# Retention's products in another order: pair of heads, block of keys, head

## The chip, the core and the metric

The kernel runs on one core of a Trainium2 chip, in one launch. A core has TensorE (matrix products), VectorE, ScalarE, GpSimd and SyncE, which work side by side and wait for each other by semaphores. The metric is the device time of one execution in microseconds. Of the kernel before there are three timed runs, and one execution more that the hardware profiler recorded.

## The reference, cut to what matters

The program computes four layers of a small language model over 512 tokens with 1024 features, in float32. The first two layers mix the tokens in three ways: retention (4 heads), an attention over selected keys, called dsa (4 heads), and a dilated attention (8 heads). Only retention is touched:

```python
RET_HEADS, HEAD_DIM = 4, 64
inner = jnp.einsum('bhncd,bhnmd->bhncm', qc, kc) * decay[None, :, None]
inner = jnp.einsum('bhncm,bhnme->bhnce', inner, vc)
...
cross = jnp.einsum('bhncd,nbhde->bhnce', qc, state_prev) * xi[None, :, None, :, None]
o = inner + cross
...
mu = jnp.mean(o, axis=-1, keepdims=True)
var = jnp.mean(jnp.square(o - mu), axis=-1, keepdims=True)
o = (o - mu) * lax.rsqrt(var + NORM_EPS) * norm_w.astype(jnp.float32)
```

For each head this is a causal product of queries with keys, times a decay that falls with the distance of the two tokens, times the values, and then a norm over the head's 64 features. The kernel computes it without the chunks: all queries that come at or after a block of 128 keys, times that block, at once.

## The kernel before, in words

Features lie on the 128 partitions and tokens along them. Two heads of 64 features share the 128 partitions: of retention's rotated queries and keys (`retqk`) head h has partitions 0 to 63 for even h and 64 to 127 for odd h, of block h // 2.

One unit of retention is a head h and a block kb of 128 keys. It goes through three steps:

- score product (line 1176, TensorE, semaphore `ret_s`): keys of the block times all queries from the block on. It uses 64 rows of TensorE's array (the head's 64 partitions) and all 128 columns. Its width w is 512 − 128 kb: 512, 384, 256 or 128. The result goes to PSUM bank 4 or 5 in turns.
- decay step (line 1480, VectorE, semaphore `ret_p`): the score times the decay table, into one of four buffers `ret_st`.
- value product (line 1184, TensorE, semaphore `ret_o`): values of the block times that buffer, accumulated over the blocks in PSUM bank 6 or 7. It uses all 128 rows and 64 columns of the array: the result has the head's 64 partitions.

Both products are in float32, and the trace shows two instructions (and two weight loads) for each. Everything else large is split into a high and a low part in a reduced format (fp32r), where a product is one instruction; line 750 (the attention's scores) and line 306 (weights times features) are of that kind.

The list `ru` (line 1062) sets the order of the 16 units. It is fixed, and all engines go through it. Retention runs beside the dsa attention, in its steps i = 6 to 14. A step of that attention on TensorE is: scores for two units in every second step (line 750), a transposition of probabilities (line 769), then what `retention(i)` adds, then the products with values (line 780). `retention(i)` issues the score products of units 2(i − 6) and 2(i − 6) + 1, and then the value products of the two units before them. VectorE's part of a step is the attention's masking (lines 823 and 829), in some steps a reciprocal and a scaling of finished results (lines 843 and 844), and then two decay steps. Retention's rotation (lines 1167, 1469, 1471) is ahead of it in steps 4 and 5, its norm in steps 15 to 17 behind it (lines 1190 and 1193). The weights come by SyncE's queue, and ScalarE and GpSimd split them (lines 260 and 269).

The waits of TensorE in this part: score product u waits for decay step u − 2, which frees its PSUM bank; value product u waits for decay step u. In both, one wait stands ahead of each product.

Of the kernel before, what the change touches and what calls it, by code (L numbers as in the profile page):

```python
# [14 lines left out]
TB = S // P  # L15
# [4 lines left out]
RET_H, DSA_H, DIL_H, FOX_H, IDX_H = 4, 4, 8, 8, 8  # L20
# [88 lines left out]
def build(nc, a, out):  # L109
    ctx = ExitStack()  # L110
    with ctx:
# [67 lines left out]
        def at(name, v):  # L179

            return sems[name], base[name] + v
# [868 lines left out]
        def first_layer(block, L):  # L1050
# [8 lines left out]
            out_a, out_b = Pace(16, 0, 3), Pace(16, 16, 7)  # L1059
            ROT, RET, GN = 4, 6, 15  # L1060
            units = [(qb, h) for qb in range(1, TB) for h in range(IDX_H)]
            ru = [(h, kb) for h in range(RET_H) for kb in range(TB)]

            @block.sync
            def _(sp):
# [26 lines left out]
            def _(pe):  # L1092
# [24 lines left out]
                for i in range(0, len(units), 2):  # L1117
                    qb, h = units[i]
# [40 lines left out]
                def retention(i):  # L1159
# [10 lines left out]
                    for u in (2 * (i - RET), 2 * (i - RET) + 1):  # L1170
                        if 0 <= u < len(ru):
                            h, kb = ru[u]
                            p0, w = HD * (h % 2), S - kb * P
                            if u >= 2:
                                pe.wait_ge(*at("ret_p", u - 1))
                            sg["ret_s"].by(pe.matmul(  # L1176
                                ps[:, 4 + u % 2, 0:w], retqk[p0:p0 + HD, 2 + h // 2, kb * P:(kb + 1) * P],
                                retqk[p0:p0 + HD, h // 2, kb * P:S], start=True, stop=True))
                    for u in (2 * (i - RET) - 2, 2 * (i - RET) - 1):
                        if 0 <= u < len(ru):  # L1180
                            h, kb = ru[u]
                            p0, w = HD * (h % 2), S - kb * P
                            pe.wait_ge(*at("ret_p", u + 1))
                            sg["ret_o"].by(pe.matmul(  # L1184
                                ps[p0:p0 + HD, 6 + h // 2, kb * P:S], retv[:, kb, h * HD:(h + 1) * HD],
                                st_b[u % 4][:, 0:w], start=kb == 0, stop=kb == TB - 1, skip_group_check=True))
# [10 lines left out]

                pe.wait_ge(*at("dq_low", 2))
                dsa.tensor(pe, retention)
                pe.wait_ge(*at("mix_lo", 6))  # L1200
                pe.wait_ge(*at("ret_lo", 2))
# [136 lines left out]
            def _(dve):  # L1338
# [121 lines left out]
                def retention(i):  # L1460
# [10 lines left out]
                            sg["ret_rotd"].by(dve.tensor_tensor(retqk[:, j, :], gn[j % 2][:], st_b[j][:], ALU.add))  # L1471
                            dve.wait_ge(*at("ret_rotd", j + 1))
                    for u in (2 * (i - RET), 2 * (i - RET) + 1):
                        if 0 <= u < RET_H * TB:
                            h, kb = divmod(u, TB)
                            w = S - kb * P
                            dve.wait_ge(*at("ret_s", u + 1))
                            if u >= 4:
                                dve.wait_ge(*at("ret_o", u - 3))
                            sg["ret_p"].by(dve.tensor_tensor(st_b[u % 4][:, 0:w], ps[:, 4 + u % 2, 0:w],  # L1480
                                                             rtab[:, T_DECAY + h * S:T_DECAY + h * S + w], ALU.mult))
# [16 lines left out]
                    if i == GN + 2:  # L1498
                        for j in range(2):
# [3 lines left out]
                                                              ALU.subtract))  # L1503

                dsa.vector(dve, retention)
                for m in range(4):
                    add_out(pl.out_b, m, 4 + m)
# [596 lines left out]
        with nc.Block() as block:  # L2104
            for L in range(DEPTH):
                first_layer(block, L)
            for layer in range(2):
                second_layer(block, layer)
# [21 lines left out]
```

## Time and profile before

| | us |
|---|---|
| timed runs | 2570.02, 2578.37, 2581.41 |
| their median | 2578.37 |
| the profiled execution | 2571.64 |
| its span in the trace | 2569.9 |
| TensorE busy | 2451.2 (95%) |
| VectorE, ScalarE, GpSimd busy | 1064.6, 944.7, 1005.7 |
| mean clock granted to TensorE | 0.975 of 2.4 GHz |

Retention's products run from 271 to 308 us of the span in the first layer and from 963 to 999 in the second. The trace's times are those of the profiled execution. A matrix product's recorded duration holds a tail in which the next one is already running, so durations of neighbours overlap and the distance of two starts says more than a duration. A granted clock of 0.50 is 1.2 GHz, 1.00 is 2.4 GHz.

### The profile page before, as it was taken

The page shows a single profiled execution, that of the slowest core. Times are in us where ns is not written, and L with a number is a line of the kernel's source. Part 1 is how long each engine was busy: PE and PEld are TensorE (multiplying, and loading weights), DVE is VectorE, ACT ScalarE, POOL GpSimd, SP SyncE. Part 2 cuts the span into 40 slices and gives each one's busy share as a digit, 9 for nine tenths or more (in the row PEclk, how much of TensorE's full clock was granted, in tenths as well). Part 3 has the DMA queues.
Part 4 walks back from the last instruction along what each step waited for, and adds up shares of the span by engine and source line. Part 5 has one row for each costly group of instructions (what it writes and reads, how often), then busy time and mean ns, then how long its engine had stood idle before and what let it go on. Part 6 is the DMA issues. An engine that isn't in the chain of part 4 may idle for free.

```text
span 2569.9 us, 29379 instructions
## 1 busy us (share of the span) xinstructions
PE 2451.2 (95%) x11844; PEld 1994.8 (78%) x11844; DVE 1064.6 (41%) x1931; ACT 944.7 (37%) x1306; POOL 1005.7 (39%) x789
## 2 busy tenths in 40 slices
PE   8988999999999889999999979899999898999997
PEld 6777588888877766888888768888888767888886
DVE  4766451221347664411224553632223766522224
ACT  5333352322343343522325333522223564422222
POOL 4422134444444230444445411354443524444442
PEclk9999899999999999999999979999999999999998
DMA  4212023233232120322323211132322312232331
GB/s 163 72 44 91 17 66 98 98 99 99 79 103 83 33 74 17 99 99 99 98 98 103 90 33 34 64 101 99 99 98 82 115 49 83 77 104 98 99 98 50
DMA packets 138279, 212.36 MB, mean 83 GB/s; under 512 B 7456, under 2 KB 65952, under 8 KB 137888
## 3 DMA queue, kind: packets, MB, share of 16 engines
q1 hardware_dynamic: 138144, 210.48, 24.7%
q8 instruction: 94, 1.54, 0.2%
q14 instruction: 41, 0.34, 0.0%
HBM read 208.36 MB, written 2.10 MB: 82 GB/s over the span
## 4 chain that ended last, share of the span: by engine, by line
PE 53%; DVE 5%; ACT 2%; issue 2%; POOL 0%; POOLq 0%; DVEq 0%; ACTq 0%
PE ps L306 45%; PE ps L331 4%; PE ps L780 1%; DVE x L653 1%; PE ps L1681 1%; PE ps L468 1%; PE ps L769 1%; DVE h_lo L543 1%; DVE tmp_both L648 0%; ACT w_hi L260 0%; PE ps L1176 0%; POOL w_lo L269 0%; PE ps L750 0%; PE ps L1184 0%; DVE ub L1899 0%
## 5 line engine op out<-in xcount | busy, mean ns | idle before, releaser
L269 POOL TENSOR_TENSOR w_lo<-raw,w_hi 128x512 fp32r<-128x512 f32 (+1 forms) x776 | 995.3, 1313 | 1528.1 <-ACT w_hi L260 1528.1
L306 PE MATMUL ps<-h_hi,w_hi 128*128 128x512 f32 x1696 | 681.2, 402 | 12.1 <-POOL w_lo L269 10.5
L306 PE MATMUL ps<-h_hi,w_lo 128*128 128x512 f32 x1696 | 663.3, 391 | 0.0
L306 PE MATMUL ps<-h_lo,w_hi 128*128 128x512 f32 x1696 | 663.3, 391 | 0.0
L260 ACT ACTIVATE w_hi<-raw 128x2048 fp32r<-128x2048 f32 (+2 forms) x196 | 363.5, 1855 | 729.1 <-PE ps L306 710.8
L306 PE MATMUL ps<-hid_hi,w_hi 128*128 128x512 f32 x992 | 392.3, 395 | 6.0 <-DVE hid_lo L851 5.1
L306 PE MATMUL ps<-hid_hi,w_lo 128*128 128x512 f32 x992 | 388.0, 391 | 0.0
L306 PEld LDWEIGHTS ps<-h_hi,w_hi 128*128 128x128 f32 x1696 | 319.5, 188 | 88.0 <-issue 21.0
L306 PE MATMUL ps<-hid_lo,w_hi 128*128 128x512 f32 x992 | 387.7, 391 | 0.0
L306 PEld LDWEIGHTS ps<-h_lo,w_hi 128*128 128x128 f32 x1696 | 319.3, 188 | 69.0 <-issue 5.6
L306 PEld LDWEIGHTS ps<-h_hi,w_lo 128*128 128x128 f32 x1696 | 319.1, 188 | 69.1 <-issue 0.4
L306 PEld LDWEIGHTS ps<-hid_hi,w_hi 128*128 128x128 f32 x992 | 187.5, 189 | 46.7 <-DVE hid_lo L851 6.3
L306 PEld LDWEIGHTS ps<-hid_hi,w_lo 128*128 128x128 f32 x992 | 187.2, 189 | 39.7
L306 PEld LDWEIGHTS ps<-hid_lo,w_hi 128*128 128x128 f32 x992 | 187.6, 189 | 38.2 <-issue 0.5
L1457 DVE TENSOR_TENSOR x<-x,ps 128x512 f32<-128x512 f32 x96 | 65.3, 685 | 290.5 <-PE ps L306 290.5
L863 ACT ACTIVATE p<-p,stat 128x128 f32<-128x128 f32 (+3 forms) x128 | 71.8, 561 | 239.0 <-DVE stat L829 238.7
L1528 DVE SCALAR_TENSOR_TENSOR tmp_both<-ps,rstd 128x512 f32<-128x512 f32 x64 | 44.1, 691 | 246.0 <-PE ps L306 222.8
L717 DVE TENSOR_TENSOR tmp_both<-ps,rstd 128x512 f32<-128x512 f32 x48 | 33.0, 690 | 247.8 <-PE ps L306 247.7
L769 PE MATMUL ps<-tab,p 128*128 128x128 f32 x320 | 64.1, 301 | 32.9 <-ACT p L863 16.9
L2089 DVE TENSOR_TENSOR acc<-acc,ps 128x512 f32<-128x512 f32 x64 | 43.8, 687 | 108.6 <-PE ps L306 108.6
L331 PE MATMUL ps<-hid_hi,w_hi 128*128 128x256 f32 x256 | 75.2, 294 | 4.3 <-issue 3.2
L823 DVE CUSTOM_DVE_ANT_0 p<-ps,tab 128x128 f32<-128x128 f32 (+3 forms) x104 | 49.3, 474 | 72.0 <-PE ps L757 30.5
(290 smaller groups left out, 2904.7 us busy)
## 6 DMA issues: line engine op xcount, KB each, us to landing
raw<-in_w_up SPq DMA_DIRECT2D x32, 1024.0 KB, 5.5
raw<-in_w_down SPq DMA_DIRECT2D x32, 1024.0 KB, 4.9
raw<-in_ffn_w_gate SPq DMA_DIRECT2D x44, 512.0 KB, 3.7
raw<-in_ffn_w_up SPq DMA_DIRECT2D x44, 512.0 KB, 4.7
raw<-in_w_in SPq DMA_DIRECT2D x20, 1024.0 KB, 4.9
raw<-in_ffn_w_down SPq DMA_DIRECT2D x20, 1024.0 KB, 4.9
raw<-in_w_out SPq DMA_DIRECT2D x8, 1024.0 KB, 4.9
raw<-in_ev_w_in SPq DMA_DIRECT2D x8, 1024.0 KB, 5.3
```

Of the source, the lines that this page charges most:

```text
L260: act.activation(w_hi[r][:, 0:slot.rows, 0:slot.width], raw[r][:, 0:slot.rows, 0:slot.width], ACT.Copy).then_inc(sems["hi_split"], 1)
L269: pool.tensor_tensor(w_lo[r][:, k, 0:slot.width], raw[r][:, k, 0:slot.width], w_hi[r][:, k, 0:slot.width].bitcast(F32), ALU.subtract).then ...
L306: mm = pe.matmul(o, lh, rh, start=first and q == 0, stop=last and q == 2, skip_group_check=True)
L331: mm = pe.matmul(o, lh, rh, start=first and q == 0, stop=last and q == 2, skip_group_check=True)
L468: mm = pe.matmul(ps[:, nm.bank, 0:S // 2], ones, two(nm.acc)[:, i, :], start=i == 0, stop=i == 1)
L717: sg["bank_free"].by(dve.tensor_tensor(o, src, rstd[:, 0:width], ALU.mult))
L769: mm = pe.transpose(ps[:, 2, kb * P:(kb + 1) * P], p_t[i % self.PB][:, kb * P:(kb + 1) * P], ident)
L823: sg["s_masked"].by(dve.tensor_tensor_reduce(out=p_t[i % self.PB][:, 0:w], in0=ps[:, e, 0:w], in1=self.bias(qb), scale=1.0, scalar=TAKEN, ...
L863: sg["p_ready"].by(act.activation(p_t[i % self.PB][:, 0:w], p_t[i % self.PB][:, 0:w], ACT.Exp, bias=sn[:, i:i + 1], scale=SCALE, accum_out ...
L1457: sg["bank_free"].by(dve.tensor_tensor(x[:, b, :], x[:, b, :], ps[:, HALF * st.groups[g].half + m, :], ALU.add))
L1528: sg["bank_free"].by(dve.scalar_tensor_tensor(out=tmp[n % 2][:], in0=ps[:, HALF * st.groups[g].half + m, :], scalar=0.0, in1=rstd[:], op0= ...
L2089: sg["bank_free"].by(dve.tensor_tensor(acc[:, b, :], acc[:, b, :], src, ALU.add))
```

## The change

The order of the units becomes pair of heads, block of keys, head. Before, head 0 went through its four blocks, then head 1, and so on: widths 512, 384, 256, 128, 512, ... Now heads 0 and 1 take turns: block 0 of head 0, block 0 of head 1, block 1 of head 0, and so on: widths 512, 512, 384, 384, ... Two neighbouring units then lie in different halves of the partitions. Each step of `retention(i)` still has two score products and two value products, now of one width each. The waits for the decay step stand only ahead of the first of the two, and ask for the later of the two numbers. VectorE takes its units from the same list instead of counting head by head.

```diff
-            ru = [(h, kb) for h in range(RET_H) for kb in range(TB)]
+            ru = [(h + e, kb) for h in range(0, RET_H, 2) for kb in range(TB) for e in range(2)]
...
                             h, kb = ru[u]
                             p0, w = HD * (h % 2), S - kb * P
-                            if u >= 2:
-                                pe.wait_ge(*at("ret_p", u - 1))
+                            if u >= 2 and u % 2 == 0:
+                                pe.wait_ge(*at("ret_p", u))
                             sg["ret_s"].by(pe.matmul(
                                 ps[:, 4 + u % 2, 0:w], retqk[p0:p0 + HD, 2 + h // 2, kb * P:(kb + 1) * P],
                                 retqk[p0:p0 + HD, h // 2, kb * P:S], start=True, stop=True))
...
                             p0, w = HD * (h % 2), S - kb * P
-                            pe.wait_ge(*at("ret_p", u + 1))
+                            if u % 2 == 0:
+                                pe.wait_ge(*at("ret_p", u + 2))
                             sg["ret_o"].by(pe.matmul(
                                 ps[p0:p0 + HD, 6 + h // 2, kb * P:S], retv[:, kb, h * HD:(h + 1) * HD],
                                 st_b[u % 4][:, 0:w], start=kb == 0, stop=kb == TB - 1, skip_group_check=True))
...
                     for u in (2 * (i - RET), 2 * (i - RET) + 1):
-                        if 0 <= u < RET_H * TB:
-                            h, kb = divmod(u, TB)
+                        if 0 <= u < len(ru):
+                            h, kb = ru[u]
                             w = S - kb * P
                             dve.wait_ge(*at("ret_s", u + 1))
```

TensorE's queue in steps 6 and 7 of the first layer, where retention's products begin (the change adds one line, so line 1184 is 1185 in the new numbering; an instruction's width is its second number, and a product stands as one row here):

```order
 L1176 MATMUL ps<-retqk 128x512 [waits ret_rotd]
-L1176 MATMUL ps<-retqk 128x384
+L1176 MATMUL ps<-retqk 128x512
 L780 MATMUL ps<-dsa_v,pT_84 128x64 [waits pT_copied]
 L780 MATMUL ps<-dsa_v,pT_84 128x64
 L769 MATMUL ps<-tab,p_79 128x128 [waits pT_copied,p_ready]
 L769 MATMUL ps<-tab,p_79 128x128 x2
-L1176 MATMUL ps<-retqk 128x256 [waits ret_p]
-L1176 MATMUL ps<-retqk 128x128 [waits ret_p]
-L1184 MATMUL ps<-ret_st_110,retv 64x512 [waits ret_p]
-L1184 MATMUL ps<-ret_st_111,retv 64x384 [waits ret_p]
+L1176 MATMUL ps<-retqk 128x384 [waits ret_p]
+L1176 MATMUL ps<-retqk 128x384
+L1185 MATMUL ps<-ret_st_110,retv 64x512 [waits ret_p]
+L1185 MATMUL ps<-ret_st_111,retv 64x512
```

The attention's rows stay where they are. Each of retention's places holds two products as before, now of one width and with one wait.

VectorE's queue in step 11, behind the reciprocal and the scaling. Before:

```order
357 L1480 TENSOR_TENSOR ret_st_112<-ps,rtab 128x256 [waits ret_o,ret_s]
358 L1480 TENSOR_TENSOR ret_st_113<-ps,rtab 128x128 [waits ret_o,ret_s]
359 L823 ISA p_78,stat<-ps,sc_95 128x384 [waits pT_ready,s_ready]
360 L823 ISA stat 128x1
361 L829 TENSOR_SCALAR stat<-stat 128x1 [waits s_masked]
```

The same place after the change:

```order
357 L1481 TENSOR_TENSOR ret_st_112<-ps,rtab 128x384 [waits ret_o,ret_s]
358 L1481 TENSOR_TENSOR ret_st_113<-ps,rtab 128x384 [waits ret_o,ret_s]
359 L823 ISA p_78,stat<-ps,sc_95 128x384 [waits pT_ready,s_ready]
360 L823 ISA stat 128x1
361 L829 TENSOR_SCALAR stat<-stat 128x1 [waits s_masked]
```

The two decay steps are wider here, and both stand ahead of the score product that TensorE issues next.

## Rows read from the trace of the kernel before

**Rows 1.** The page: busy time of each engine, us (share of the span), instructions.

```profile
PE 2451.2 (95%) x11844; PEld 1994.8 (78%) x11844; DVE 1064.6 (41%) x1931; ACT 944.7 (37%) x1306; POOL 1005.7 (39%) x789
```

**Rows 2.** Timeline of PE, second layer: start, length, instructions merged, idle before.

```profile
968.67 2.98 PE L1184 MATMUL ps<-ret_st,retv 128*64 128x512 f32 x4
...
984.75 0.92 PE L1176 MATMUL ps<-retqk 64*128 64x256 f32 x4
985.59 1.72 PE L1184 MATMUL ps<-ret_st,retv 128*64 128x512 f32 x4
987.24 1.10 PE L780 MATMUL ps<-dsa_v,pT 128*128 128x64 f32 x8
...
989.69 1.77 PE L1176 MATMUL ps<-retqk 64*128 64x512 f32 x4 [0.26 <-DVE ret_st L1480]
...
998.11 0.86 PE L1184 MATMUL ps<-ret_st,retv 128*64 128x256 f32 x4
...
1000.15 0.52 PE L769 MATMUL ps<-tab,p 128*128 128x128 f32 x3 [0.60 <-ACT p L863]
```

**Rows 3.** Stretches: start:end length, PE busy, granted clock, DMA share, GB/s.

```profile
271.40:295.30 23.90, 23.90 (x60) 0.50 0.14 44
...
964.30:971.10 6.80, 6.80 (x18) 0.51 0.47 154
971.10:999.00 27.90, 27.03 (x136) 1.00 0.00 1
```

**Rows 4.** Timeline of DVE in steps 6, 11 and 12; what DVE waited for at L1480.

```profile
274.15 0.56 DVE L1480 TENSOR_TENSOR ret_st<-ps,rtab 128x384 f32<-128x384 f32 x1 [0.59 <-PE ps L1176]
...
304.21 0.20 DVE L843 RECIPROCAL stat<-stat 128x8 f32<-128x8 f32 x1 [4.39 <-PE ps L780]
304.45 0.69 DVE L844 TENSOR_TENSOR on<-ps,stat 128x512 f32<-128x512 f32 x1
305.06 0.61 DVE L1480 TENSOR_TENSOR ret_st<-ps,rtab 128x256 f32<-128x256 f32 x2
...
306.68 1.20 DVE L1480 TENSOR_TENSOR ret_st<-ps,rtab 128x512 f32<-128x512 f32 x2 [0.36 <-PE ps L1176]
...
  PE ps L1176: 17.3, 15
```

**Rows 5.** Line 1176: what its engine sat idle for: us, times.

```profile
  DVE ret_st L1480: 1.5, 4
```

**Rows 6.** Timeline at retention's start, PE and its weight loads (PEld), both layers.

```profile
963.25 2.23 PE L1176 MATMUL ps<-retqk 64*128 64x512 f32 x4 [2.18 <-DVE retqk L1471]
...
271.12 2.99 PE L1176 MATMUL ps<-retqk 64*128 64x512 f32 x4 [2.18 <-DVE retqk L1471]
...
271.78 0.33 PEld L1176 LDWEIGHTS ps<-retqk 64*128 64x128 f32 x1 [0.36 <-issue]
...
272.63 0.33 PEld L1176 LDWEIGHTS ps<-retqk 64*128 64x128 f32 x1 [0.52 <-issue]
```

**Rows 7.** Timeline of PE and its weight loads in the first layer's step 12.

```profile
305.52 1.77 PE L1176 MATMUL ps<-retqk 64*128 64x512 f32 x4 [0.26 <-DVE ret_st L1480]
...
306.06 0.19 PEld L1176 LDWEIGHTS ps<-retqk 64*128 64x128 f32 x1 [0.24 <-issue]
...
306.49 0.19 PEld L1176 LDWEIGHTS ps<-retqk 64*128 64x128 f32 x1 [0.24 <-issue]
```

**Rows 8.** Groups by form, whole run: xcount, busy us, mean ns, idle before.

```profile
L1184 PE MATMUL ps<-ret_st,retv 128*64 128x512 f32 x16 | 11.3, 794 | 0.0
```

**Rows 9.** Timeline of PE: attention's score pairs (L750), whole-array products (L306).

```profile
252.01 0.40 PE L306 MATMUL ps<-hid_hi,w_lo 128*128 128x512 f32 x1
252.24 0.39 PE L306 MATMUL ps<-hid_hi,w_hi 128*128 128x512 f32 x1
...
267.46 0.39 PE L750 MATMUL ps<-hid_lo,dsaq_hi 64*128 64x512 f32 x2
267.69 0.40 PE L750 MATMUL ps<-hid_hi,dsaq_lo 64*128 64x512 f32 x2
```

## The prediction

> **What bounds the kernel now.** I read the page's busy times first: TensorE is busy 95% of the span and no other engine half of it [rows 1]. So a change to TensorE's own work counts in full, wherever TensorE is the engine waited for. The next view is the timeline of TensorE in the stretch where retention's products run. A step there is a run of products, one behind the other: in the second first_layer the products of scores with keys start at 984.75, those with values at 985.59, the attention's own products at 987.24, and between them nothing is idle [rows 2]. In the 27.9 us from 971.1 to 999 TensorE is busy for 27.03 [rows 3]. VectorE, which multiplies the decay in between, sits idle 17.3 us in all until a score product comes, while the score products sat idle for it only 1.5 us in both layers together [rows 4, 5]. So TensorE is what is waited for, and a step costs the time that its products stream.
>
> The view of stretches gives the clock. TensorE streams at half of its full speed (1.2 instead of 2.4 GHz) from 271.4 to 295.3 in the first layer's retention, and from 964.3 to 971.1 in the second's [rows 3]. Ahead of both lies an idle time of 2.18 us until VectorE has rotated the keys [rows 6]. The stretch from the first score product to the seventh pair of them is 305.52 − 271.12 = 34.4 us in the first layer and 989.69 − 963.25 = 26.4 us in the second [rows 2, 6, 7]: the same work, 8.0 us apart by the clock alone.
>
> **What a product costs.** Each float32 product is two instructions (16 instructions of each width on each of the two lines, for 8 products in two layers; one width stands) [rows 8]. Weight loads are issued as soon as the instruction ahead starts to stream, so their pitch is the streaming time. It is 306.49 − 306.06 = 0.43 us for 512 columns at full clock [rows 7] and 272.63 − 271.78 = 0.85 us at half clock [rows 6]. A product of 512 columns is 0.86 us, and narrower ones go down in proportion. A head has widths 512, 384, 256 and 128, 2.5 units of 512; four heads and two lines make 20 units a layer, 17.2 us at full clock.
>
> **The change, part by part.**
>
> *The order.* So far two neighbouring products belong to one head. They use the same 64 partitions of keys and queries (the score product) or the same 64 partitions of the result (the value product), and so the same half of the array: four instructions in a row, A0 A1 A0' A1'. Now the neighbours are heads h and h+1, in different halves: A0 A1 B0 B1, both of one width. Can B0 run beside A1? The trace shows it for the reduced-precision products of the attention's scores, whose two heads alternate between the same two halves: two products of 512 columns come every 267.69 − 267.46 = 0.23 us, where one product over the whole array comes every 252.24 − 252.01 = 0.23 us [rows 9]. Two for the time of one. There the order is A B A B, all pairs overlap. Here the two instructions of a head follow each other, A1 has to wait for A0 (0.43 apart above), and B0 is behind A1 in the queue. So of four unit times three are left: the saving is a quarter. For the value products, which split the array by its columns of results instead of its rows, no row shows an overlap. The bounds are nothing (float32 instructions of two halves do not overlap) and a half (B0 gets past A1, and all pairs overlap as in rows 9). I take the quarter: it is the overlap of rows 9 with the order in the queue that the weight loads of rows 7 show.
>
> The sum: a quarter of 17.2 is 4.3 us a layer, 8.6 in both. At half clock a unit costs double. The first layer's slow stretch holds score products 0 to 7 and value products 0 to 5, (2560 + 2176)/512 = 9.25 units; a quarter of 0.86 on top of each is 2.0 us. The second's holds score products 0 to 3 and value products 0 and 1, 4.25 units, 0.9 us. Together **11.5 us**.
>
> The Trainium skill says in "TensorE: Matmul & The Clock Gate", Part 3, that matmuls start and end strictly in program order, which gives the same three of four. The same part says that a weight load overlaps a running matmul only where the row group differs. This trace differs: the loads at 306.06 and 306.49 start while a product of the same rows streams, and no gap follows. If the rule held for value products, which all use all rows, they would not overlap; that is the rival "scores only" below, and its time is worked out from rows there.
>
> *The waits.* TensorE's score product u waited for VectorE's step u−2, and the value product u for step u. Now the first of a pair waits for the second's step too, and the second has no wait. The waits taken away were met already, but for fractions of a microsecond: TensorE's idle time before value products is 0 in the view by form, of which one width stands and the other three read alike [rows 8]. I put their removal at nothing. One wait gets stricter: score product 2k must wait for VectorE's step 2k−1, not 2k−2. Where does that show? In most steps TensorE has 1.7 us or more of value products and attention work between [rows 2]. At one step it doesn't: behind the attention's eighth value group VectorE does a reciprocal, 0.20, and a scaling, 0.69, and only then the two decay steps at 305.06, and TensorE starts at 305.52, after an idle time of 0.26 [rows 4, 7]. Now both steps must be done, and both are 384 wide instead of 256 and 128. A lone 384 takes 0.56 [rows 4] and the pair 512 and 384 takes 1.20 [rows 4], so a second begins some 0.64 behind a first of 512 and about 0.5 behind one of 384: the pair ends at 305.06 + 0.5 + 0.56 = 306.1, and TensorE starts at 306.15 instead of 305.52. That is **0.65 us more, in each layer, 1.3 in all**. Behind TensorE's wait stand only its own next products, which all come later by as much. The bounds are 0.15 us (the two steps run wholly beside each other, 305.06 + 0.56) and 0.8 (they take the 1.20 of a 512 and a 384).
>
> *The last step.* At 998.11 TensorE has the last two value products (256 and 128 wide, now 128 and 128), and waits at 1000.15 for ScalarE's exponential, 0.60 us [rows 2]. What is saved here goes into that wait: 0.2 us a layer, **0.4 in all**.
>
> *Everything else.* VectorE's 32 decay steps keep their widths and number, in another order. SyncE's and GpSimd's queues are not touched: no transfer moves. The group norm behind it starts from the end of the last value product and comes earlier with it.
>
> **The sum.** 11.5 − 1.3 − 0.4 = 9.8 us. The profiled execution took 2571.64 us, so by its clock 2561.8. The three timed runs were 2570.02, 2578.37 and 2581.41; with the profiled one their mean is 2575.4. The spread of 11 us is of the size of one slow stretch like the first layer's (8.0 above), and I take it for that, without a row that shows it. The changed kernel has the same lottery, so I set the gain against the mean: 2575.4 − 9.8 = 2565.6, **2566 us**. It is 12 below the median of 2578.37.
>
> **The rivals.**
>
> *Scores only* (0.15). Only the halves split by rows overlap, the value products don't. For: no row shows the other kind. Against: nothing but its absence. The saving is half of 8.6, and of the extra 5 and 2.5 units at half clock, 1.1 and 0.5: 5.9, less 1.7, is 4.2: 2571 us.
>
> *No overlap, and the stricter wait* (0.12). This ends on the slower side. Float32 instructions of two halves run one after the other (rows 9 show another precision), and the change leaves only the stricter wait: 1.3 us at the step after the reciprocal. In addition the first pair, now 512 and 512, is 2 × (0.85 − 0.64) = 0.4 us longer at half clock before its decay step can start. It decides as soon as the overlap is under 0.1 us a pair, since there are 16 pairs a layer. 2575.4 + 1.7 = 2577 us. "The change doesn't do what it says" is the same case.
>
> *The clock comes back early* (0.15). With both halves at work, the first layer's slow stretch might end as early as the second's did, after some 7 us instead of 24 [rows 3]. For: in the second layer the clock rose at 971.1, in the run of value products that starts at 968.67 [rows 2, 3], and such a run now has both halves of the array at work. Against: it is shorter now. It gives 8.0 less the 1.4 of the extra saving at half clock that goes, 6.6 on top of the forecast where it happens, in most of the executions: 2560 us.
>
> *The clock stays low longer* (0.08). Runs of products without a gap become shorter while the fixed work between them stays, and the second layer's slow stretch becomes as long as the first's: 8.0 − 1.1 = 7 us: 2573 us.
>
> The forecast keeps 0.50, with a range of its own of 2560 to 2572 for the lottery. Half a per cent, 12.9 us, is about what a measurement of this kernel can tell from no change. Against a median like the one shown, the line is at 2565.5; against the mean, at 2562.5. Of the forecast's 0.50 I give 0.20 to faster, of the early clock nearly all, and little of the rest: 0.36. Slower by half a per cent needs no overlap and a long slow stretch at once, 0.04. The remaining 0.60 is no difference. The range has to take in the early clock and part of an overlap by halves below (twice the 11.5 would give 2554), and no overlap above: 2555 to 2579.
>
> **What would show it.** Right: in a score pair of 512 columns at full clock the third weight load comes with the second instead of 0.43 behind, and the pair takes three units (1.3 us and the tail) instead of four; the value pairs do the same; the wait of line 1176 for VectorE's decay step grows to about 0.9 at the step after the reciprocal; TensorE's busy time falls by some 10 us. Wrong: pitches of 0.43 throughout (no overlap), value pairs of four units (scores only), or a slow stretch in the first layer that ends near 280 or goes on past 300.

## The result, and the profile after

| | before | after |
|---|---|---|
| timed runs, median | 2578.35 us (2570.02 to 2581.41, 4 runs) | 2549.66 us (2544.71 to 2551.03, 4 runs) |
| ratio of the times | | 0.989, 95% interval 0.9864 to 0.9917 |
| profiled execution | 2571.64 us | 2544.71 us |
| TensorE busy | 2451.2 us | 2420.9 us |

The changed kernel is faster by 1.1%. The forecast was 2566 us with a range of 2555 to 2579: the direction was right, the size was not, and the time lies below the range. In later comparisons the changed kernel gave 0.9905 (0.9871 to 0.9938) and 0.9899 (0.9876 to 0.9923).

The page of the changed kernel, busy time of the engines, against [rows 1]:

```profile
span 2542.9 us, 29379 instructions
PE 2420.9 (95%) x11844; PEld 1975.9 (78%) x11844; DVE 1064.0 (42%) x1931; ACT 944.5 (37%) x1306; POOL 1006.1 (40%) x789
```

Only TensorE's time fell, by 30 us, with the same number of instructions.

The timeline of TensorE in the first layer's steps 10 to 12 (start, length, instructions merged, idle before), against [rows 2, 7]:

```profile
284.59 1.13 PE L1176 MATMUL ps<-retqk 64*128 64x512 f32 x4
285.65 0.44 PE L1185 MATMUL ps<-ret_st,retv 128*64 128x128 f32 x4
...
288.02 1.08 PE L1185 MATMUL ps<-ret_st,retv 128*64 128x512 f32 x4
289.03 1.10 PE L780 MATMUL ps<-dsa_v,pT 128*128 128x64 f32 x8
...
292.08 0.70 PE L1176 MATMUL ps<-retqk 64*128 64x256 f32 x4 [0.86 <-DVE ret_st L1481]
```

Four instructions of 512 columns start at 284.59 and the next group starts at 285.65, 1.06 us later. Before, two of 512 and two of 384 took from 989.69 [rows 2] to 991.39, where the value products began, 1.70 us:

```profile
991.39 0.86 PE L1184 MATMUL ps<-ret_st,retv 128*64 128x256 f32 x4
```

Two units of 0.43 us and 0.2 for the change of groups make 1.06; the three units that I forecast would have made 1.5. The value products do the same, in 1.01 us: 288.02 to 289.03. So both halves run wholly beside each other.

Weight loads of the same score pair, against [rows 7], and of the value pair at 288.02:

```profile
284.59 0.30 PEld L1176 LDWEIGHTS ps<-retqk 64*128 64x128 f32 x4
...
288.02 0.20 PEld L1185 LDWEIGHTS ps<-ret_st,retv 128*64 128x64 f32 x4 [0.55 <-issue]
```

All four loads of the score pair lie within 0.30 us, and those of the value pair within 0.20. Before, the third came 0.54 us behind the first and the fourth 0.97 behind.

The granted clock in stretches of the changed kernel (length, then busy times of PE, PEld, DVE, ACT and POOL, granted clock), against [rows 3]:

```profile
271.30:278.10 6.80, 6.80 (x23) 3.07 (x19) 3.24 (x10) 2.38 (x6) 0.41 (x1) 0.50 0.45 154
278.10:300.00 21.90, 19.54 (x135) 11.62 (x136) 11.48 (x39) 7.34 (x22) 0.00 (x0) 1.00 0.01 1
947.10:953.90 6.80, 6.80 (x23) 2.87 (x19) 3.36 (x10) 2.38 (x6) 0.53 (x1) 0.50 0.46 154
```

The first layer's stretch at half clock lasts 6.8 us instead of 23.9. The second layer's has its old length.

What the score products' engine sat idle for (us, times), in the view of line 1176, against [rows 5]:

```profile
  DVE retqk L1472: 9.2, 4
  DVE ret_st L1481: 4.6, 6
```

And what VectorE sat idle for ahead of its decay steps, against the last of [rows 4]:

```profile
  PE ps L1176: 9.1, 10
```

TensorE waits more for VectorE, and VectorE less for TensorE. The view of line 1176 counts the idle time ahead of a product and that ahead of its weight load one by one: of the 4.6 us TensorE's products alone make 1.7 (0.86 in each layer), and of the 1.5 us of [rows 5] they make 0.5.

**The sum of the two traces.** I measure a layer from the first product of the rotation (line 1167) to the first mean product of the norm (line 1190, now 1191). Everything between is the stretch that the change touches. Before:

```profile
262.48 1.88 PE L1167 MATMUL ps<-retqk,tab 128*128 128x512 f32 x4
...
316.34 1.88 PE L1190 MATMUL ps<-gn,tab 128*128 128x512 f32 x4
...
954.61 1.88 PE L1167 MATMUL ps<-retqk,tab 128*128 128x512 f32 x4
...
1000.51 1.88 PE L1190 MATMUL ps<-gn,tab 128*128 128x512 f32 x4
```

After:

```profile
261.99 1.88 PE L1167 MATMUL ps<-retqk,tab 128*128 128x512 f32 x4
...
300.30 1.88 PE L1191 MATMUL ps<-gn,tab 128*128 128x512 f32 x4
...
937.91 1.88 PE L1167 MATMUL ps<-retqk,tab 128*128 128x512 f32 x4
...
976.23 1.88 PE L1191 MATMUL ps<-gn,tab 128*128 128x512 f32 x4
```

That is 53.86 and 45.90 us before, and 38.31 and 38.32 after: 15.5 us in the first layer and 7.6 in the second, 23.1 of the 26.9 us between the two profiled executions. The rest lies outside these stretches: 0.5 ahead of the first, and the other 3 in parts of the program that are the same in both. There the clock fell at other places in the two executions: by the mean granted clocks of 0.975 and 0.982 TensorE had 129 us at half clock before and 92 after, and only 17 of the 37 lie in retention. What the other 20 cost is not worked out here.

### The profile page after: what moved, and what is told of

Its sections match the earlier page's. It is cut to its first block, busy times and chain, and to the rows that moved or that the text cites. A ratio compares the mean times of both kernels' runs of the same rounds, so it can differ in the third digit from the quotient of the medians.

```text
span 2542.9 us, 29379 instructions
## 1 busy us (share of the span) xinstructions
PE 2420.9 (95%) x11844; PEld 1975.9 (78%) x11844; DVE 1064.0 (42%) x1931; ACT 944.5 (37%) x1306; POOL 1006.1 (40%) x789
## 4 chain that ended last, share of the span: by engine, by line
PE 53%; DVE 5%; ACT 2%; issue 2%; POOL 1%; POOLq 0%; DVEq 0%; ACTq 0%
PE ps L306 45%; PE ps L331 4%; PE ps L780 1%; DVE x L653 1%; POOL w_lo L269 1%; PE ps L1682 1%; PE ps L468 1%; PE ps L769 1%; ACT w_hi L260 1%; DVE h_lo L543 0%; DVE tmp_both L648 0%; PE ps L750 0%; DVE ub L1900 0%; DVE ssum L457 0%; DVE macc L637 0%
## 5 line engine op out<-in xcount | busy, mean ns | idle before, releaser
L306 PE MATMUL ps<-h_hi,w_hi 128*128 128x512 f32 x1696 | 681.3, 402 | 12.3 <-POOL w_lo L269 10.5
L306 PE MATMUL ps<-h_hi,w_lo 128*128 128x512 f32 x1696 | 663.3, 391 | 0.0
L306 PE MATMUL ps<-h_lo,w_hi 128*128 128x512 f32 x1696 | 662.9, 391 | 0.0
L306 PE MATMUL ps<-hid_hi,w_hi 128*128 128x512 f32 x992 | 392.0, 395 | 6.0 <-DVE hid_lo L851 5.1
L306 PEld LDWEIGHTS ps<-h_hi,w_hi 128*128 128x128 f32 x1696 | 319.7, 189 | 87.9 <-issue 21.1
L306 PE MATMUL ps<-hid_hi,w_lo 128*128 128x512 f32 x992 | 387.8, 391 | 0.0
L306 PE MATMUL ps<-hid_lo,w_hi 128*128 128x512 f32 x992 | 387.7, 391 | 0.0
L306 PEld LDWEIGHTS ps<-h_lo,w_hi 128*128 128x128 f32 x1696 | 319.4, 188 | 69.2 <-issue 5.7
L306 PEld LDWEIGHTS ps<-h_hi,w_lo 128*128 128x128 f32 x1696 | 318.8, 188 | 69.3 <-issue 0.4
L306 PEld LDWEIGHTS ps<-hid_hi,w_hi 128*128 128x128 f32 x992 | 187.3, 189 | 46.6 <-DVE hid_lo L851 6.3
L306 PEld LDWEIGHTS ps<-hid_hi,w_lo 128*128 128x128 f32 x992 | 187.3, 189 | 39.7
L306 PEld LDWEIGHTS ps<-hid_lo,w_hi 128*128 128x128 f32 x992 | 187.4, 189 | 38.1 <-issue 0.5
L769 PEld LDWEIGHTS ps<-tab,p 128*128 128x128 f32 x320 | 38.1, 153 | 53.1 <-ACT p L863 34.3
```

The source lines that it names most:

```text
L306: mm = pe.matmul(o, lh, rh, start=first and q == 0, stop=last and q == 2, skip_group_check=True)
L769: mm = pe.transpose(ps[:, 2, kb * P:(kb + 1) * P], p_t[i % self.PB][:, kb * P:(kb + 1) * P], ident)
```

## Experiments

Each run is told by its median, its ratio to the kernel before with the 95% interval, and the length of a layer as just measured. The stretch at half clock in the retention of each layer is given beside it.

**The changed kernel once more, and the kernel before once more.** No edit.

> The changed kernel once more. Theory (both halves run wholly side by side): 2549 us again, within 4; in the trace the first score product to the first mean product of the norm takes 29.6 us in both first layers, with a slow stretch of about 7 us in each. Rival (the first layer's short slow stretch was luck of one execution): the stretch there is 20 us or more this time, and the time is 2552 or above.

Measured: 2548.57 us; 38.29 us in both layers, 6.8 us at half clock in each. As the theory said.

> The kernel before once more, for a second trace. My prediction took the 11 us between its runs for slow stretches of the clock. If so, a run near 2578 has some 14 us more at half clock than the profiled one (which had 129 us of it in all), and a run near 2570 has the same. If the difference lies elsewhere, the sum at half clock stays at 129 us whatever the time.

Measured: 2568.89 us. The rotation to the norm took 45.90 us in the first layer and 53.86 in the second, the other way round than in the first trace:

```profile
262.05 1.88 PE L1167 MATMUL ps<-retqk,tab 128*128 128x512 f32 x4
...
307.95 1.88 PE L1190 MATMUL ps<-gn,tab 128*128 128x512 f32 x4
...
945.38 1.88 PE L1167 MATMUL ps<-retqk,tab 128*128 128x512 f32 x4
...
999.24 1.88 PE L1190 MATMUL ps<-gn,tab 128*128 128x512 f32 x4
```

By its mean granted clock of 0.977 TensorE had 118 us at half clock in all, where the expectation had the first trace's 129 for a run near 2570; the two executions are 2.75 us apart.

In these two traces a layer before has one of two lengths, 8.0 us apart. The 51 runs of the kernel before in the three comparisons lie in three groups with nothing between them: 2 runs at 2562 to 2564 us, 22 at 2567 to 2574, 27 at 2578 to 2584. Both traces with one long layer are of the middle group. I take the groups for none, one and two long layers; that would be 1.5 long layers on average, 12 us. No trace shows two long layers. The clocks recorded with the runs fit, though: 0.980 in the lowest group, 0.975 to 0.978 in the middle one, 0.971 to 0.975 in the highest. By them TensorE had 102, 120 and 139 us at half clock on average, steps of 18 and 19 where a long stretch in place of a short one makes 17.

**The order alone.**

```diff
-                            if u >= 2 and u % 2 == 0:
-                                pe.wait_ge(*at("ret_p", u))
+                            if u >= 2:
+                                pe.wait_ge(*at("ret_p", u - 1))
...
-                            if u % 2 == 0:
-                                pe.wait_ge(*at("ret_p", u + 2))
+                            pe.wait_ge(*at("ret_p", u + 1))
```

> The new order of units with the waits of before: one ahead of each product. Theory 1 (order alone makes the overlap, a wait that is met costs nothing): value pairs and score pairs start together as in the changed kernel, time 2548 to 2550; at the one step where the second decay step is late the first score product starts earlier by 0.5 us but the pair is split. Theory 2 (a wait between the two products, even a met one, keeps the second head's product from starting beside the first): the pairs go one after the other, the time is that of before, 2570 to 2580.

Measured: 2548.57 us, 0.9906 (0.9874 to 0.9937); 38.31 us in both layers. Its timeline:

```profile
286.53 1.13 PE L1176 MATMUL ps<-retqk 64*128 64x512 f32 x4
287.59 0.44 PE L1184 MATMUL ps<-ret_st,retv 128*64 128x128 f32 x4
...
293.56 1.16 PE L1176 MATMUL ps<-retqk 64*128 64x256 f32 x4 [0.39 <-DVE ret_st L1480]
294.65 0.87 PE L1184 MATMUL ps<-ret_st,retv 128*64 128x384 f32 x4
```

The pair of 512 takes 1.06 us here too, so a wait that is met does not keep the halves apart. The one wait that is not met does: the pair of 256 starts 0.47 us earlier than the merged wait allows (0.39 idle instead of 0.86), and takes 1.16 instead of 0.70. Both ways give the same length. The order is the whole gain.

The weight loads of this split pair also show what order the program gives: both loads of the first head, then the wait, then both of the second.

```profile
293.56 0.29 PEld L1176 LDWEIGHTS ps<-retqk 64*128 64x128 f32 x2 [0.63 <-DVE ret_st L1480]
294.03 0.29 PEld L1176 LDWEIGHTS ps<-retqk 64*128 64x128 f32 x2 [0.17 <-DVE ret_st L1480]
```

**The waits alone.** The same edit the other way round, in the kernel before.

> The order of before with the merged waits: the first of each two products waits for both decay steps, the second for none. Both theories: no overlap, as both products lie in the same half of the array, so 2575 to 2580, the same as before; my prediction puts the removed waits at nothing and the stricter one at a few tenths a layer here (the second decay step is 128 wide where it matters).

Measured: 2570.49 us, 0.9986 (0.9964 to 1.0008), no difference. The median is below the forecast of 2575 to 2580, as is that of the kernel before beside it, 2572.41. In its trace both layers have the short stretch of 6.8 us and last 46.10 us (in the first, 264.29 to 310.39), against 45.90 before at the same stretch: the merged waits cost 0.2 us a layer by themselves. The profiled execution, with two short stretches, took 2564.67 us, the lowest group's time. Three of the ten runs are at 2564 to 2565 us, against 2 of 51 before. Whether the waits alone make long stretches rarer is not settled by so few.

**The value products in one half.**

```diff
-                                ps[p0:p0 + HD, 6 + h // 2, kb * P:S], retv[:, kb, h * HD:(h + 1) * HD],
+                                ps[0:HD, 6 + h // 2, kb * P:S], retv[:, kb, h * HD:(h + 1) * HD],
```

> The changed kernel with the value products of odd heads written to partitions 0 to 63 as well, so that both value products of a pair use the same 64 columns of the array (the odd heads' results are left out of the output). Only score pairs can overlap. If the overlap is whole in both kinds, the value products stream 4.3 us a layer longer than in the changed kernel, 8.6 in both at full clock, up to 12 if the slow stretch in the first layer grows: 2558 to 2562. If value pairs overlapped by a quarter only: 2553 to 2555.

Measured: 2556.87 us, 0.9933 (0.9911 to 0.9955), 1 us below the forecast for a whole overlap and 8.3 above the changed kernel's 2548.57; 42.57 and 42.34 us a layer, 4.1 more than the changed kernel at the same 6.8 us at half clock. In its timeline the score pair is as short as in the changed kernel and the value pair is not:

```profile
291.90 0.92 PE L1176 MATMUL ps<-retqk 64*128 64x384 f32 x4
292.74 1.93 PE L1185 MATMUL ps<-ret_st,retv 128*64 128x512 f32 x4
```

1.93 us instead of 1.08: two units more. The overlap of two halves by columns is whole, and worth 4.1 us a layer. In this run the two products of a pair also write the same partitions of PSUM; which of the two, columns or partitions, keeps them apart was not tried.

**The score products in one half.**

```diff
-                                ps[:, 4 + u % 2, 0:w], retqk[p0:p0 + HD, 2 + h // 2, kb * P:(kb + 1) * P],
-                                retqk[p0:p0 + HD, h // 2, kb * P:S], start=True, stop=True))
+                                ps[:, 4 + u % 2, 0:w], retqk[0:HD, 2 + h // 2, kb * P:(kb + 1) * P],
+                                retqk[0:HD, h // 2, kb * P:S], start=True, stop=True))
```

> The changed kernel with the score products of odd heads taken from partitions 0 to 63 as well (the even head's scores stand in for the odd head's). Only value pairs can overlap. The score products stream 4.3 us a layer longer: 2558 to 2562, the same as with the value products in one half. If the score pairs give the larger part, it is slower than the run with the value products in one half.

Measured: 2591.83 us, 1.0064 (1.0042 to 1.0086): slower than the kernel before, and 30 us above the forecast's range. It is slower than the run with the value products in one half, too, but not for the reason that the forecast gives there. The stretches tell why:

```profile
272.80:324.00 51.20, 51.13 (x160) 28.34 (x159) 15.96 (x51) 10.55 (x29) 0.45 (x1) 0.50 0.07 21
972.50:1020.30 47.80, 47.73 (x145) 25.82 (x143) 12.91 (x41) 8.86 (x25) 0.72 (x1) 0.50 0.07 23
```

TensorE was busy almost without a gap and at half clock through nearly the whole of both retentions, and the layers took 59.9 and 59.8 us. The value products did overlap:

```profile
1010.83 2.07 PE L1176 MATMUL ps<-retqk 64*128 64x256 f32 x4
1012.83 1.55 PE L1185 MATMUL ps<-ret_st,retv 128*64 128x384 f32 x4
1014.31 0.69 PE L780 MATMUL ps<-dsa_v,pT 128*128 128x64 f32 x2
```

Four score instructions of 256 take 2.00 us and four value instructions of 384 only 1.48. What the value products saved came back several times over through the clock: all seven runs are at 2588.71 to 2593.97 us, and the median is 25 us above that of the run below, which has no overlap at all. Why the clock stays low here is open.

**Both in one half.** Both edits.

> Both of these at once: order, widths and waits of the changed kernel, and no two products in different halves. If the overlap is the whole cause, this is the kernel before plus the stricter wait: 2575 to 2582, pitches of 0.43 us between all instructions of 512 columns, and first layers of 34 to 45 us. If the new order or the merged waits gain by themselves (or through the clock), it stays below 2568. It also shows how long the slow stretches last without overlap.

Measured: 2566.43 us, 0.9969 (0.9948 to 0.9989); 48.30 us in both layers, with 10.2 us at half clock in each. It came out below the 2575 to 2582 forecast for the overlap as the whole cause, and below the 2568 under which something else was to gain as well. That was the clock: the forecast had counted on layers with a long stretch; its trace has none, and all ten runs are at 2563.52 to 2569.63 us. At half clock half the time is lost, so 10.2 instead of 6.8 us costs 1.7 us. Without that a layer takes 46.6 us, as against 46.1 with the waits alone. At an equal clock the new order has no gain by itself when the products share a half:

```profile
293.56 1.98 PE L1176 MATMUL ps<-retqk 64*128 64x512 f32 x4
295.48 0.65 PE L1185 MATMUL ps<-ret_st,retv 128*64 128x128 f32 x4
```

1.92 us from one group to the next: four units.

**Unequal pairs.**

```diff
-            ru = [(h + e, kb) for h in range(0, RET_H, 2) for kb in range(TB) for e in range(2)]
+            ru = [(h + e, TB - 1 - kb if e else kb) for h in range(0, RET_H, 2) for kb in range(TB) for e in range(2)]
...
-                                st_b[u % 4][:, 0:w], start=kb == 0, stop=kb == TB - 1, skip_group_check=True))
+                                st_b[u % 4][:, 0:w], start=u % 8 < 2, stop=u % 8 > 5, skip_group_check=True))
```

> The changed kernel with the odd head's key blocks in the reverse order, so that a pair is 512 beside 128, 384 beside 256, and so on (the sums of odd heads are started at another block, so their output is left out). It tells how the second head gets beside the first. If the four instructions run as A0 B0 A1 B1 in a fixed order, B1 starts with A1, 0.43 us behind A0, although B0 (128 wide, 0.11 us) is long done. If B overtakes freely, B1 starts 0.11 us behind B0. In both cases a pair takes the time of its wider product: 512, 384, 384, 512 instead of 512, 384, 256, 128, so 512 columns more for each two heads and kind of product, 3.4 us a layer: 2554 to 2558. If the overlap needed equal widths, the pairs go one after the other: 2563 or above.

Measured: 2573.2 us, 0.9989 (0.9965 to 1.0012), above the forecast, and where it had put pairs that go one after the other. They do not. The question is answered in the trace, by the view by form of the first pair's instructions running in two short stretches, 271.25 to 271.50 and 271.55 to 271.62:

```profile
L1176 PE MATMUL ps<-retqk 64*128 64x512 f32 x1 | 0.7, 693 | 2.2 <-DVE retqk L1472 2.2
L1176 PE MATMUL ps<-retqk 64*128 64x128 f32 x2 | 0.5, 322 | 0.0
...
L1176 PE MATMUL ps<-retqk 64*128 64x512 f32 x2 | 1.1, 641 | 2.2 <-DVE retqk L1472 2.2
```

In the first stretch both instructions of the narrow head have started and only one of the wide head. The wide head's second one comes after. So the second head's instructions pass the first head's second one, although that stands ahead of them in the program. VectorE's wait shows that their signals do not pass:

```profile
272.21 0.89 DVE L1481 TENSOR_TENSOR ret_st<-ps,rtab 128x512 f32<-128x512 f32 x2 [0.29 <-PE ps L1176]
```

The narrow head's two instructions had both started by 271.50, and VectorE was free at 271.92, ready for the first signal of the pair. It started at 272.21, when the wide head's product was done. So the count of finished products rose in program order here, and VectorE's wait for its number was enough.

The time missed for the clock again: the first layer had 44.3 us at half clock, and lasted 56.8 us. The second had 13.7 and lasted 44.5; with 6.8 it would be 41.1, as against 38.3 + 3.4 = 41.7 worked out from the wider products. The ten runs spread from 2561.76 to 2587.84 us, with granted clocks from 0.978 down to 0.965.

**The decay steps ahead of the reciprocal.** In VectorE's loop over the attention's steps:

```diff
+                    early = i == 11 and n == 16
+                    if early:
+                        beside(i)
...
-                    beside(i)
+                    if not early:
+                        beside(i)
```

> The changed kernel with VectorE's two decay steps of step 11 ahead of the reciprocal and scaling of the attention. The stricter wait at that step, 0.86 us of idle time before line 1176 in each layer, goes: 1.7 us less in all, 2547 to 2548, if nothing else is late there. Rival: the next wait (the attention's results, which come 1 us later) takes its place, and the time stays at 2549 to 2550.

Measured: 2552.27 us, 0.9906 (0.9874 to 0.9937), and 37.38 us in both layers, 0.93 less than the changed kernel. The idle time for VectorE in the view of the score products' line fell from 4.6 us to 0.7 (the line is 1180 and the decay step 1485 here). What is left stands ahead of weight loads; ahead of the products themselves the 1.7 us are gone:

```profile
  DVE ret_st L1485: 0.7, 2
```

The stretch gained what was forecast. The time did not show it, and its median is above both the forecast and the rival's 2549 to 2550: five runs spread from 2544.24 to 2553.51, and the two kernels' intervals are alike. A gain of 1.9 us is below what these runs can tell.

**Three rotated blocks instead of four.** On top of the last one:

```diff
                     if i == RET:
+                        pe.wait_ge(*at("ret_rotd", 3))
+                    if i == RET + 4:
                         pe.wait_ge(*at("ret_rotd", 4))
```

> The changed kernel with VectorE's decay steps of step 11 ahead of the reciprocal (as in decay_first) and, new, the first score product waiting for three of the four rotated blocks; the fourth holds keys of heads 2 and 3 and is waited for four steps later. In the new order the first four steps use heads 0 and 1 alone. The 2.2 us of idle time ahead of the first score product shrinks to under 1 us: 1.5 us less a layer, 3 in all. Theory 1 (the clock falls because of that idle time): the slow stretch of 6.8 us in each layer goes too, 3 us more a layer: 2541 to 2544. Theory 2 (the work around it is thin enough by itself): the slow stretch stays: 2545 to 2548.

Measured: 2546.69 us, 0.9876 (0.9853 to 0.9899), 2537.25 to 2551.28. In its trace a layer lasts 34.93 us, 2.45 less than before this edit, and no stretch at half clock is left:

```profile
262.00:297.00 35.00, 29.99 (x184) 1.00 0.10 31
934.40:969.30 34.90, 29.88 (x183) 1.00 0.10 31
```

The idle time did not go, though. It moved behind the first score pair, to the next transposition:

```profile
268.51 1.13 PE L1182 MATMUL ps<-retqk 64*128 64x512 f32 x4 [0.51 <-DVE retqk L1478]
269.57 0.66 PE L780 MATMUL ps<-dsa_v,pT 128*128 128x64 f32 x4
272.43 0.52 PE L769 MATMUL ps<-tab,p 128*128 128x128 f32 x3 [2.19 <-ACT pT L876]
```

So in this execution an idle time of 2.2 us alone did not make the clock fall; the same amount at another place left it up, in both layers. The profiled execution was one of the fast ones, at 2540.14 us, 1 us below theory 1's range. The median lies where theory 2 had put it, and the clocks recorded with the six runs go from 0.985 in the fastest to 0.978 in the slowest: in the slower ones the clock fell more. Where, no trace shows.

**Products in the gap.** On top of that:

```diff
                     if i == RET:
+                        pe.wait_ge(*at("ret_rotd", 1))
+                        for _ in range(2):
+                            pe.matmul(ps[:, 4, :], rot_m, retqk[:, 0, :], start=True, stop=True)
                         pe.wait_ge(*at("ret_rotd", 3))
```

> As rot_three, with two more products of 512 columns over the whole array (a rotation repeated into a bank that is free, its result unused) issued as soon as the first block is rotated. They take 1.7 us of TensorE, about what is left of the idle time. If idle time in the array is what lets the clock fall, the slow stretch goes: 2541 to 2544, or 0 to 1 us behind rot_three if that has lost it already. If not, it only adds its own time: 1 to 2 us behind rot_three.

Measured: 2540.13 us, 0.9855 (0.9828 to 0.9882), 2537.46 to 2541.67; a layer lasts 34.92 us, the same as without them:

```profile
270.47 1.88 PE L1175 MATMUL ps<-retqk,tab 128*128 128x512 f32 x4
272.28 1.13 PE L1185 MATMUL ps<-retqk 64*128 64x512 f32 x4
```

Its stretches, all at full clock:

```profile
264.20:299.00 34.80, 31.44 (x188) 1.00 0.10 31
936.60:971.50 34.90, 31.52 (x188) 1.00 0.09 31
```

The added products lie in the idle time and cost nothing. All four runs are below all six of the changed kernel on the same chip. This version, which leaves nothing out of the computation, is faster than both kernels. Of the 8.5 us to the changed kernel, 6.8 are in the traces: 3.4 a layer, 0.9 by the decay steps and 2.5 by the wait for three blocks. That the two products add anything is not shown: the layers are as long as without them, the profiled executions took 2540.09 and 2540.14 us, and the two intervals overlap.

**The changed kernel on that chip.**

> The changed kernel beside these three, for the comparison on one chip: 2546 to 2551, with 29.65 us from the first score product to the norm's first product in both layers, and a slow stretch of 6.8 us in each.

Measured: 2548.6 us, 0.9899 (0.9876 to 0.9923), but the profiled execution took 2560.13 us and had 20.4 us at half clock in both layers, which lasted 44.5 us each:

```profile
273.60:294.00 20.40, 20.34 (x76) 11.10 (x76) 6.16 (x21) 5.02 (x15) 0.00 (x0) 0.50 0.16 52
...
956.20:976.50 20.30, 20.24 (x76) 11.14 (x76) 6.05 (x21) 5.07 (x15) 0.00 (x0) 0.50 0.16 53
```

This is the rival that stood beside the first repetition of the changed kernel. The changed kernel has the long stretch too, only less often: of its 15 runs in all, 3 are above 2554 us, with the lowest granted clocks of the 15, 0.975 to 0.977.

## Why the prediction was wrong in size

The forecast was 2566 us and the measured time 2549.7, 16 us lower. Two steps failed: the size of the overlap, and the base.

**The order: the first step that failed.** "B0 is behind A1 in the queue. So of four unit times three are left: the saving is a quarter." The four instructions do not keep their order. Each half of the array takes its own next instruction, as the unequal pair shows, so A0 runs with B0 and A1 with B1. Two units of four are left and the saving is a half, 8.6 us a layer at full clock instead of 4.3. I had named this as the upper bound and put it aside on the strength of the weight loads of [rows 7]. Those loads belonged to one half and could say nothing on a second one. The Trainium skill's sentence on strict program order ("TensorE: Matmul & The Clock Gate", Part 3), which I had taken as agreeing, does not hold here for starts: an instruction of 128 columns starts ahead of one of 512 that precedes it. For the signals of finished products, which are what a wait sees, this case shows program order. With this step alone put right, at the 7.6 us a layer that the traces show, the forecast would have been 2575.4 − 15.2 = 2560 us, inside the range. (The prediction's 2554 for a whole overlap counts an extra saving at half clock as well, which did not come.)

**The extra saving at half clock, 2.9 us: a term of the wrong kind.** I let the slow stretch hold the same products and counted them double. In the second layer it kept its length instead, 6.8 us before and after, although it held 23 of TensorE's instructions instead of 18. So that layer lost the same 3.4 us both times, and the whole of the layer's gain comes from the sum at full clock: 8.6, less the two waits. In the first layer the stretch became shorter, which is the rival's mechanism. It is also in part the draw of the profiled executions, since the second trace of the kernel before has its long stretch in the other layer.

**The stricter wait, 1.3 us: right.** The idle time at the step behind the reciprocal is 0.86 us instead of 0.26, in each layer: 1.2. The two decay steps took 1.01 us; I had put 1.06.

**The last step, 0.4 us: about right.** The wait for the exponential grew from 0.60 to 0.90 us, 0.6 in both layers. With these, a layer should gain 8.6 − 0.6 − 0.3 = 7.7 us at an equal clock. The trace has 45.90 − 38.32 = 7.6.

**The waits taken away, nothing: right.** The order alone gives the whole gain, the waits alone 0.2 us a layer of loss.

**The base: the second step that failed.** I took the spread between runs of the kernel before for slow stretches, without a row. The two traces and the clocks of the 51 runs bear that out: a stretch is long or short, 8.0 us apart. But then I wrote "The changed kernel has the same lottery, so I set the gain against the mean". It does not have the same. The kernel before has some 1.5 long stretches in an average run, 12 us. In two of the changed kernel's three traces both stretches are short, and 12 of its 15 runs are at 2544 to 2551 us, near those two. By subtraction this accounts for the 10 us between the 2560 above and the measured 2549.7, as against 5 for the overlap (15.2 instead of 9.8). Why long stretches became rarer is open.

**The idle time of the score products, 1.5 us: misread.** [rows 5] count weight loads as well. Ahead of the products themselves it is 0.5 us in both layers. The conclusion, that TensorE is what is waited for, gets stronger by it.

**The rivals.** *Scores only*: excluded, since the value products give 4.1 us a layer. The Trainium skill's rule on weight loads ("TensorE: Matmul & The Clock Gate", Part 3) spoke for it. The four loads of the value pair, all of them for the same rows, lie within 0.20 us at 288.02 and speak against it. *No overlap*: excluded. *The clock comes back early* got 0.15, and a short stretch stood beside the larger overlap in most executions, by their times: 8.0 us in the first layer of the profiled one, as priced. It was no rival but a second term. That it is "both halves at work" that ends a stretch is not shown: with neither kind of product paired it ended after 10.2 us. *The clock stays low longer*: seen in one of three traces, 20.4 us in both layers.

Together: 7.6 us twice is 15.2, and some 12 us for the 1.5 long layers that an average run before has. That is 27 us, less what the changed kernel's own long stretches cost. The ratios give 24 to 28.

**What stays open.** Why the clock stays low for 6.8 us in one execution and for 20 or more in another of the same kernel isn't settled, nor what ends a stretch. The runs show only which work it went with.

## What to carry to other kernels

Small float32 products that use half of TensorE's array, by rows or by columns, should alternate between the halves: two of them then take the time of one, and neither the two-instruction form of float32 nor a wait that is already met is in the way. An upper bound that the engine could reach should stay in the range until a row for that very case excludes it, and two rivals that can hold at once need their sum in it: here the whole overlap and short stretches together were what came. And a kernel whose clock falls has a second price list: a saving in TensorE's work can be lost to the clock (the run with the score products in one half), and moving an idle time to another place can gain, 2.45 us a layer in the one trace where the clock then stayed up.

## What the runs showed that I had not expected

- Instructions of the two halves start out of program order: in the unequal pair, two of 128 columns had started when only one of 512 had. The pair's first signal still came only at 272.2, with the wide product done.
- The clock over the same sequence of work differed with how the halves are filled. At half clock in the two layers: 51.2 and 47.8 us with only the value products paired, 10.2 and 10.2 with neither, 6.8 and 6.8 with only the score products paired, 6.8 and 6.8 with both (20.4 and 20.3 in one execution of three), 44.3 and 13.7 with both in unequal pairs, 23.9 and 6.8 in the kernel before. It also differs between executions of one kernel, so a single trace says little; the first two kinds are apart in all their runs, seven above 2588 us and ten below 2570.
- An idle time of 2.2 us ahead of the first score pair went with a fallen clock in every trace that had it, twelve with two layers each. The same idle time one step later left the clock at full speed, in both layers of one trace.
